# Rotary partners of the first block fetched by transfers between partitions, and the probabilities of a unit turned after the next unit's scores

## The reference, cut to what matters

```
u = rms_norm(h, attn_norm[l])
dq, dk, dv, rq, rk, rv, rg, gq, gk, gv, gate_logits = split(u @ w_in[l])
dq = partial_rope(rms_norm(dq, diff_q_norm[l]))     # 4 heads, two maps of 64
dk = partial_rope(rms_norm(dk, diff_k_norm[l]))
rq, rk = apply_rope(rq), apply_rope(rk)             # 4 heads of 128, no norm
gq = axial_rope(rms_norm(gq, gqa_q_norm[l]))        # 8 query heads of 64
gk = axial_rope(rms_norm(gk, gqa_k_norm[l]))        # 2 key heads of 64
# apply_rope(x): [x1*c - x2*s, x2*c + x1*s], x1 and x2 the halves of x
# partial_rope: only the first 16 of 64 features; axial_rope: 32 by row, 32 by column
```

## Time and profile before

| | us |
|---|---|
| median of three runs | 3668.25 (3666.96 to 3669.92) |
| profiled execution, own time | 3669.73 |
| its span, first to last instruction | 3667.9 |
| mean granted TensorE clock | 0.997 of 2.4 GHz |
| PE busy | 3579.5 (98%) |
| DVE busy | 1718.9 (47%) |
| ACT busy | 1390.4 (38%) |

### The profile page before, as it was taken

The page is one execution under the profiler, slowest core; times in us unless marked ns, Lnnn a source line. Parts: engine busy times, 40 slices in busy tenths (PEclk is TensorE's granted clock), DMA queues, the critical chain, the costliest instruction groups (busy, mean ns, idle before and its releaser), DMA issues.

```text
span 3667.9 us, 47289 instructions
## 1 busy us (share of the span) xinstructions
PE 3579.5 (98%) x18053; PEld 2684.7 (73%) x18053; DVE 1718.9 (47%) x2498; ACT 1390.4 (38%) x2056; POOL 2.4 (0%) x9
## 2 busy tenths in 40 slices
PE   8999999999999999999999899999999999999999
PEld 5565788777775656887777764488888885368998
DVE  5664434434456754344333545543333355644334
ACT  4554323322245543233222334533323334443334
POOL 0000000000000000000000000000000000000000
PEclk9999999999999999999999999999999999999999
DMA  3111233555531112334565320012222222013332
GB/s 113 46 46 41 71 96 92 155 149 143 156 91 46 47 41 69 92 111 135 161 174 149 91 66 3 2 51 64 63 63 63 63 78 72 3 46 97 93 92 86
DMA packets 571967, 304.71 MB, mean 83 GB/s; under 512 B 26592, under 2 KB 565552, under 8 KB 571824
## 3 DMA queue, kind: packets, MB, share of 16 engines
q1 hardware_dynamic: 571168, 302.41, 29.0%
q10 hardware_dynamic: 656, 0.33, 0.0%
HBM read 299.55 MB, written 2.10 MB: 82 GB/s over the span
## 4 chain that ended last, share of the span: by engine, by line
PE 94%; ACT 2%; DVE 2%; issue 1%; DMA 0%; SPq 0%; DVEq 0%; ACTq 0%
PE ps L1085 14%; PE ps L1087 14%; PE ps L1086 14%; PE ps L1404 10%; PE ps L1406 10%; PE ps L1408 10%; PE ps L1597 2%; PE ps L1579 2%; PE ps L1254 2%; PE ps L1285 2%; PE ps L1169 1%; PE ps L1266 1%; PE ps L1238 1%; PE ps L1538 1%; PE ps L1282 1%
## 5 line engine op out<-in xcount | busy, mean ns | idle before, releaser
L1761 ACT ACTIVATE whi<-wraw 128x1024 fp32r<-128x1024 f32 x448 | 470.7, 1051 | 545.9 <-DMA wraw<-in_w_mlp 247.1
L1085 PE MATMUL ps<-uhi,whi 128*128 128x512 f32 (+1 forms) x1456 | 626.2, 430 | 12.1 <-DVE ulo L2413 5.0
L2396 DVE TENSOR_TENSOR wlo<-wraw,whi 128x1024 fp32r<-128x1024 f32 x448 | 546.0, 1219 | 117.4 <-ACT whi L1761 112.7
L1086 PE MATMUL ps<-ulo,whi 128*128 128x512 f32 (+1 forms) x1456 | 572.8, 393 | 0.0
L1087 PE MATMUL ps<-uhi,wlo 128*128 128x512 f32 (+1 forms) x1456 | 572.7, 393 | 0.0
L1085 PEld LDWEIGHTS ps<-uhi,whi 128*128 128x128 f32 x1456 | 274.4, 188 | 136.0 <-issue 71.3
L1086 PEld LDWEIGHTS ps<-ulo,whi 128*128 128x128 f32 x1456 | 274.8, 189 | 77.3 <-issue 22.8
L1087 PEld LDWEIGHTS ps<-uhi,wlo 128*128 128x128 f32 x1456 | 274.0, 188 | 65.4
L1404 PE MATMUL ps<-u2hi,whi 128*128 128x512 f32 (+1 forms) x1216 | 295.5, 320 | 3.6 <-DVE wlo L2396 2.4
L1404 PE MATMUL ps<-yhi,whi 128*128 128x512 f32 (+1 forms) x976 | 295.7, 353 | 0.0
L1408 PE MATMUL ps<-yhi,wlo 128*128 128x512 f32 (+1 forms) x976 | 295.0, 353 | 0.0
(11 more groups left out here) (323 smaller groups left out, 4629.0 us busy)
## 6 DMA issues: line engine op xcount, KB each, us to landing
wraw<-in_w_in SPq DMA_DIRECT2D x128, 512.0 KB, 3.8
wraw<-in_w_mlp SPq DMA_DIRECT2D x128, 512.0 KB, 4.0
mod_raw<-in_w_mod SPq DMA_DIRECT2D x96, 512.0 KB, 5.3
wraw<-in_w_mlp_in SPq DMA_DIRECT2D x64, 512.0 KB, 4.3
wraw<-in_w_mlp_out SPq DMA_DIRECT2D x64, 512.0 KB, 3.9
wraw<-in_w_branch SPq DMA_DIRECT2D x16, 512.0 KB, 3.4
wraw<-in_w_out SPq DMA_DIRECT2D x16, 512.0 KB, 3.8
wraw<-in_w_o SPq DMA_DIRECT2D x16, 512.0 KB, 3.8
```

Of the source, the lines that this page charges most:

```text
L1085: pe.matmul(bank, whs[:, i], x_hi[:, k], start=(i == 0), stop=False)
L1086: pe.matmul(bank, whs[:, i], x_lo[:, k], start=False, stop=False)
L1761: act.activation(whi[:, r], wraw[:, r], ACT.Copy).then_inc(w_hi, 1)
L2396: dve.tensor_tensor(wlo[:, r], wraw[:, r], whi[:, r].bitcast(F32), ALU.subtract).then_inc(w_split, 1)
```

## The change

For each rope, PE's "rotate" step and its permutation matrices are gone. When ACT has copied a projection to `rawb`, SP sends the partner features to a new tile `rotated` by transfers between partitions: 4 transfers of 8 partitions for a diff rope, 4 of 32 for a gqa rope (whose features are now ordered so that row and column parts lie together), 2 of 64 for a ret rope. They stand in SP's program behind the load of the weight chunk four places on. SP first waits for the copy and, because there is one tile `rotated`, for the rope before to be finished.

Normed ropes are reordered on DVE: gain and cosine on `rawb`, swapped gain and signed sine on `rotated` ("head_scale", now at end + 3.1, two instructions), then their sum, then the multiplication by the root ("roped", now at end + 3.7). Plain ropes keep three DVE instructions at end + 2.4 instead of end + 0.9, and read the partners from `rotated` instead of from a bank. One small transfer (`gain_swapped`) comes first among the parameters, and POOL clears `rotated` once per layer.

The other part of the change moves "turn" from place + 2.6 (+ 3.3 for the second) to + 2.9 (+ 3.6), which is behind the score step of the next unit (at + 2.85); "turned" and "attend" move along.

```
+SWAPS = [[(at + n * (1 - half), at + n * half, n) for at in starts for half in range(2)]
+         for starts, n in (((0, 64), 8), ((0,), 64), ((0, 64), 32))]
...
     def turn_about(end, r):
...
-            put(at + 0.9, "head_scale", rope=r)
-            at += 2
-        put(at, "rotate", rope=r)
-        put(at + 0.4, "roped", rope=r)
+            at += 2.3 if end == ends[0] + 1 else 0
+            put(at + 1.6, "head_scale", rope=r)
+            at += 2.2
+        else:
+            at += 1.9
+        put(at, "roped", rope=r)
...
             for m in range(2 if kind == "gqa" else 1):
-                s = put(at + 2.6 + 0.7 * m, "turn", score=unit, index=m)
-                put(at + 2.9 + 0.7 * m, "turned", head=s, score=unit, index=m)
-        at += 4.2
+                s = put(at + UNIT_SPACE + 0.05 + 0.7 * m, "turn", score=unit, index=m)
+                put(at + UNIT_SPACE + 0.35 + 0.7 * m, "turned", head=s, score=unit, index=m)
+        at += UNIT_SPACE + 1.45
...
+                def rotations(chunk):
+                    if chunk not in ropes_of:
+                        return
+                    r = ropes_of[chunk]
+                    bank_done(sp, bank_evac, r.tile)
+                    sp.wait_ge(rope_done, r.rot)
+                    sp.wait_ge(rotated_clear, l + 1)
+                    for to, start, n in SWAPS[r.table]:
+                        sp.dma_start(rotated[to:to + n, :], rawb[start:start + n, r.n % 2, :]).then_inc(rot_in, 16)
...
                             column_chunk(whole.chunk, a["w_in"][l], whole.columns)
+                        rotations(whole.chunk - RAW)
...
-                    elif step.name == "rotate":
-                        r = step.rope
-                        if r.normed:
-                            pe.wait_ge(qn_ready, r.norm + 1)
-                        else:
-                            bank_done(pe, bank_evac, r.tile)
-                        bank_wait(pe, aux_free, r.rot_aux)
-                        src = rawb[:, r.n % 2]
-                        pe.matmul(ps[:, AUX + r.rot_aux % 2], mats[:, r.table, :], src, start=True, stop=True)\
-                            .then_inc(rot_done, 1)
...
                     elif step.name == "head_scale":
                         r = step.rope
-                        inverse_root(r.root)
                         bank_done(dve, bank_evac, r.tile)
-                        dve.scalar_tensor_tensor(rawb[:, r.n % 2], rawb[:, r.n % 2], par[:, r.gain:r.gain + 1],
-                                                 root[:, r.root % 2], ALU.mult, ALU.mult).then_inc(qn_ready, 1)
+                        dve.wait_ge(rot_in, 16 * r.rot_in)
+                        src, swapped = rawb[:, r.n % 2], r.gain - ROW["diff_q_norm"]
+                        dve.scalar_tensor_tensor(src, src, par[:, r.gain:r.gain + 1], ropes[:, 2 * r.table], ALU.mult,
+                                                 ALU.mult)
+                        link(dve.scalar_tensor_tensor(rotated[:, :], rotated[:, :], gain_swapped[:, swapped:swapped + 1],
+                                                      ropes[:, 2 * r.table + 1], ALU.mult, ALU.mult))
                     elif step.name == "roped":
                         r = step.rope
+                        src = rawb[:, r.n % 2]
                         if r.normed:
-                            dve.wait_ge(qn_ready, r.norm + 1)
+                            link(dve.tensor_tensor(t1, src, rotated[:, :], ALU.add))
+                            inverse_root(r.root)
                         else:
                             bank_done(dve, bank_evac, r.tile)
-                        src = rawb[:, r.n % 2]
-                        link(dve.tensor_tensor(t1, src, ropes[:, 2 * r.table], ALU.mult))
-                        dve.wait_ge(rot_done, r.rot + 1)
-                        dve.tensor_tensor(t2, ps[:, AUX + r.rot_aux % 2], ropes[:, 2 * r.table + 1], ALU.mult)\
-                            .then_inc(aux_free[r.rot_aux % 2], 1)
-                        bank_done(dve, aux_free, r.rot_aux)
+                            link(dve.tensor_tensor(t1, src, ropes[:, 2 * r.table], ALU.mult))
+                            dve.wait_ge(rot_in, 16 * r.rot_in)
+                            link(dve.tensor_tensor(t2, rotated[:, :], ropes[:, 2 * r.table + 1], ALU.mult))
...
-                        dve.tensor_tensor(dst, t1, t2, ALU.add).then_inc(rope_done, 1)
+                        if r.normed:
+                            dve.tensor_tensor(dst, t1, root[:, r.root % 2], ALU.mult).then_inc(rope_done, 1)
+                        else:
+                            dve.tensor_tensor(dst, t1, t2, ALU.add).then_inc(rope_done, 1)
```

More of the change, by code:

```diff
@@ L107, in rope @@
     def rope(dst, slot, table, hd=None, gain=None):
-        return Step("rope", dst=dst, slot=slot, table=table, hd=hd, gain=gain)
+        r = Step("rope", dst=dst, slot=slot, table=table, hd=hd, gain=gain)
+        r.normed = gain is not None
+        return r
     def turn_about(end, r):
@@ L222, in number_steps @@
             if s.use in ("normed", "plain"):
-                s.rope.n, s.rope.tile, s.rope.normed = num["rope"](), s.tile, s.use == "normed"
+                s.rope.n, s.rope.tile = num["rope"](), s.tile
             if s.use == "normed":
@@ L234, in number_steps @@
             s.rope.root = num["root"]()
-        elif name == "head_scale":
-            s.rope.norm = num["normed"]()
-        elif name == "rotate":
-            s.rope.rot_aux, s.rope.rot = num["aux"](), num["rot"]()
         elif name == "roped":
             r = s.rope
+            r.rot = num["rot"]()
+            r.rot_in = num["rot_in"](len(SWAPS[r.table])) + len(SWAPS[r.table])
             r.free_after = 0 if r.hd is None else last.get(("scored", r.hd - 2), 0)
@@ L503, in __init__ @@
             "rank_normed "
-            "gqa mean split final gate norm norm_tile mlp_tile residual x_turn").split()}
+            "gqa rot_in mean split final gate norm norm_tile mlp_tile residual x_turn").split()}
         last = {"value_turn": -1, "swish_tile": -1, "final": -1}
@@ L676, in build @@
         decay = sb("decay", [P, TOEPLITZ], scope=head_scope)
+        rotated = sb("rotated", [P, SEQ], scope=head_scope)
         head_scope.close()
@@ L751, in build @@
         shifts = sb("shifts", [P, 2, 2])
+        gain_swapped = sb("gain_swapped", [P, 4 * DEPTH])
         token_root = sb("token_root", [P, 4])
@@ L976, in half_chunk @@
                     sp.dma_start(view[1], second).then_inc(raw_in[r], 16)
+                ropes_of = {step.chunk: step.rope for step in s.heads if step.name == "project" and step.rope}
+                def rotations(chunk):
[7 more added lines that the diff above has]
+                        sp.dma_start(rotated[to:to + n, :], rawb[start:start + n, r.n % 2, :]).then_inc(rot_in, 16)
                 for step in s.heads:
@@ L1001, in _ @@
                                          w.rearrange("(k p) c -> p k c", p=P)).then_inc(raw_in[r], 16)
+                        rotations(step.chunk - RAW)
                     elif step.name == "gate":
                         column_chunk(step.chunk, a["w_in"][l], GATES + D * step.n + P * step.d)
+                        rotations(step.chunk - RAW)
                 for j in range(KT):
@@ L1136, in small_products @@
                 pe.wait_ge(small_sums, 1)
-                pe.matmul(ps[:, SCORE + 1, 0:4], mats[:, 4, :], small[:, 16:20], start=True, stop=True)\
+                pe.matmul(ps[:, SCORE + 1, 0:4], mats[:, 1, :], small[:, 16:20], start=True, stop=True)\
                     .then_inc(par_turned, 1)
@@ L1290, in _ @@
                         bank_wait(pe, aux_free, step.aux)
-                        pe.matmul(ps[:, AUX + step.aux % 2], mats[:, 4, :], fo[:, :], start=True, stop=True)\
+                        pe.matmul(ps[:, AUX + step.aux % 2], mats[:, 1, :], fo[:, :], start=True, stop=True)\
                             .then_inc(mean_done, 1)
@@ L1295, in _ @@
                         bank_wait(pe, aux_free, step.aux)
-                        pe.matmul(ps[:, AUX + step.aux % 2], mats[:, 4, :], fsq[:, :], start=True, stop=True)\
+                        pe.matmul(ps[:, AUX + step.aux % 2], mats[:, 1, :], fsq[:, :], start=True, stop=True)\
                             .then_inc(fsq_used, 1)
@@ L1974, in _ @@
                         act.wait_ge(sq_used, r.sq + 1)
[L1975 removed]
+                        root_of(r.root, r.sum_aux, 64, NORM_EPS, (rope_done, r.rot + 1))
                     elif step.name == "value_turned":
@@ L2376, in small_parameters @@
                     link(dve.tensor_scalar(c, c, factor, None, ALU.mult))
+                for at in (0, 2 * DEPTH):
+                    link(dve.tensor_scalar(gain_swapped[:, at:at + DEPTH], gain_swapped[:, at:at + DEPTH], 64 ** -0.5, None, ALU.mult))
                 dve.wait_ge(small_exp, 2)
@@ L3027, with swapped, axes_apart @@
 SECOND_DMAS = 5
-PARAM_DMAS = 11 + 2 + 1 + 8 + 4 + 4
```

(16 more changed lines are left out.)

35 lines of the change are left out of this document (18 added, 17 removed).

## The result

| | before | after |
|---|---|---|
| median | 3669.09 us (3666.96 to 3670.05, 4 runs) | 3633.63 us (3632.98 to 3636.19, 4 runs) |
| profiled span | 3667.9 us | 3632.3 us |
| mean granted clock | 0.997 | 0.997 |

A forecast was written before the change was run, and what follows sets the result against it. PE, busy 98% of the span, was taken as the bound. Terms -36.1 - 2.8 - 7.7 - 5.1 - 2.0 + 7.8 + 1.6 + 3.8 sum to -40.5 us, so 3668.25 becomes 3628 us, range 3612 to 3651.

The forecast's parts named there:

- The rotates: On PE in the attention stage: 42 rotates at 0.86 us each leave, -36.1 us, with 43.8 as upper bound.
- waits ahead of rotates: PE's waits for DVE ahead of rotates go together with the rotates, -2.8 us.
- behind copies: PE's turns waiting for the bank behind a copy (3.5 and 1.6 us) no longer wait, -5.1 us.
- Waits for probabilities: PE's turns waiting for weighed probabilities: 3.4 us left in place of 11.1, -7.7 us.
- New neighbours: Steps now touching in one bank on PE: ten pairs of turns +7.8 us, two value turns touching a diff turn +1.6.
- gqa value turn and attend: One value turn and one attend per layer wait for the second "turned" behind ACT's exponentials: +3.8 us, bounds 0 and 8.
- the attend's move: One attend per layer on PE depends on the later second "turned" in gqa units: 0.7 us more each, within the +3.8.
- Transfers taken at 0: Partner transfers on SP land before DVE wants them, covered by 2.0 us or at worst 0.4: no cost.
- Rival 3: Partners come late at DVE's wait on `rot_in`, passed on to PE from 0.96 us per rope: 3678 at 1.2; chance 0.05.
- Rival 1: Waits moved, not removed: eight DVE ropes cost PE 1.5 us each, new neighbours wait twice as long; 3649, chance 0.22.
- the turns' move: Turns on PE put behind the next scores: shorter waits against new neighbours and gqa order, -1.6 us net.
- Rival 4: Longest new waits of PE bring the 1.2 GHz clock, adding 4 to 8 us: 3634, inside the forecast's 0.58 chance.

The follow-up runs named there:

- the doubled rotates: Kernel before with each of the 42 rotate products issued twice into the same bank: 3702.81 us, ratio 1.0098 to the kernel before.
- The parted turns: Changed kernel with the attend step back at + 4.2 and the ten touching pairs of turns parted: 3628.01 us, on another chip 3624.21 us.
- ropes alone: Changed kernel with turn, turned and attend steps at their old places, new transfers and rope order kept: 3657.65 us, ratio 0.9970 to the kernel before.
- cut transfers: Changed kernel with every transfer of partners cut into two halves along the tokens: 3653.06 us, ratio 0.9956 to the kernel before.
- turns alone: Kernel before with turn, turned and attend steps moved as in the change, rotates kept: 3661.72 us, ratio 0.9982 to the kernel before.
- the kernel with more products: Changed kernel with turns at their old place and the product summing a normed rope's squares issued twice, 26 more products: 3671.80 us.

## Why the prediction was right, and where its steps were off

The forecast of 3628 (3612 to 3651) against 3633.6 was right in sign and size, and inside its range. The main mechanism, rotates leaving a busy PE, is as forecast; that the total came so near is in part luck. The sum had -4.4 us for all waits together and the rows give +4.8 (39.1 against 34.3), 9.2 us worse. Some 4 us of PE's own time that the sum did not have were gained by the new order. By its own steps:

- **The rotates** (-36.1): right; the doubled rotates give 34.5.
- **The waits ahead of rotates** (-2.8), **behind copies** (-5.1), **of retention scores** (-2.0): gone, gone, and -2.7.
- **Waits for probabilities** (-7.7): mis-sized by 1.8; 5.2 us are left, not 3.4, and over the sign that the prediction named (below 4). For the first unit the working gave 1.2 to 1.3 and the trace shows 1.02, but six more waits of up to 1.0 stood in units to which I gave 0.4 per layer.
- **New neighbours** (+7.8 + 1.6): all there to the number (7.9 and 1.6). The parted turns show the first to be worth 9.6: the price was the wait in the row, not the time from start to start.
- **gqa value turn and attend** (+3.8): +1.8 and +2.7 come to 4.5.
- **The step that was off most: the attend's move**, taken at +0.7 per layer for PE alone. What I left out is ACT's order behind it: moved by 0.1 place, "attended" of the last pair fell behind the copy of a projection whose end was 6 us off. +6.0 in the trace; undone, 6.7 by medians and 4.2 by spans. It is two thirds of the 9.2 us by which the waits were off; another 1.2 us are waits of the last norms for ACT's `fsq` (they are there with ropes alone too), which the sum did not have either.
- **Transfers taken at 0**: right for this kernel (7.7 us of DVE's waits, nothing of it traced on to PE beyond the 5.2), with a cover of about 1 us and not 2.0. Rival 3 put the price of lateness as "passed on to PE, from 0.96 us per rope on"; cut transfers passed on 19.4 / 42 = 0.46 us per rope, mostly at the first unit of each layer and by the clock.
- **Rival 1** (waits moved, 1.5 us for each of eight ropes) is wrong for the changed kernel. Something like it happens with the ropes alone: 27.6 us of waits in 24 places. So the term that the sum had for the turns' move, -1.6 net, hides what it did: with the new ropes on DVE it is worth 3657.65 - 3633.63 = 24.0 us (two chips), without them 6.6. With it the rotates can go without waits opening in their place.
- **Rival 4** (clock): nothing in the changed kernel (10.2 us before, 10.3 after), some 8 us in the ropes alone and 7 in the cut transfers.

The waits and the rotates at 0.82 give -34.4 + 4.8 = -29.6 of the -35.6 between the two spans. The rest lies in PE's work by starts. Take each stretch of PE's other work in the attention stages, from its start to the start of the second projection product behind it, less 0.23 us and without waits. All stretches together fall from 309.9 to 269.5 us, and -40.4 + 4.8 = -35.6. The rotates are 36.1 of the 40.4, at 0.86 each. The other 4.3 (up to 1 of it is the clock) come from the new order: turn, scores and the return to projections take 69.88 - 67.96 - 0.23 = 1.69 us before, while scores, turn and the return take 107.06 - 105.27 - 0.23 = 1.56. Before, 42 turns stood directly ahead of scores, and now none does. With turns alone the same count falls by 5.0 us, which with the waits (31.1 against 34.3) and the clock (7.1 against 10.2) makes up the -11.5 between those spans.

What stays open: no kernel with the ropes split on DVE as before the change, and none with products added where the rotates stood, was run, so the two halves of the waits with ropes alone are counted from the traces and not tested one by one.

## What to carry to other kernels

Price the parts of a change together where one engine's order and another's slack meet: work taken off the bound engine shows its gain only if what it then waits for was given room in the same step. When a step is moved by a tenth of a place in a hand-written order, read on each engine what it falls behind, above all an instruction that waits for something long. And price a wait between two neighbours from start to start of the work around it, not from the wait's row.

## What the runs showed of the hardware

The same stall does not always bring the lower clock. With ropes alone, 2.08 us of idle PE ahead of 68.29 were followed by half the clock (1.98 us for a score step of 1.13); in the kernel with more products, the same place has the same wait of 2.08, the same 2.92 busy of 5.00 us, and a granted clock of 1.00. Over runs this goes with spread: for the ropes alone the fastest run (3653.36 us) has a mean granted clock of 0.997 and the slowest (3663.14) 0.993. The Trainium skill ("TensorE: Matmul & The Clock Gate", section on how oscillation bites) has long idle gaps throttle the engine again; the wait of 4.05 us, with a granted clock of 0.50 behind it, agrees, while the waits of 2.08 us, halving the clock in one kernel and not in another, do not follow from the gap alone.

A wait's row is less than what it costs: 0.78 us in the row, 1.05 from the start of the pair to the start of the next product, since the record of the turn before it reaches 0.25 us past the point where the next product starts if nothing waits (0.66 us long, next product 0.41 later, in the parted pair). The Trainium skill ("Perfetto Trace Analysis", section on the Tensor Engine instruction) says that the profiler estimates a matmul's end; the trace agrees.

The order of short steps on PE has a price of its own, with no wait in it: a turn ahead of scores takes 1.69 us to the return of the projections' pace (67.96 to 69.88 before), behind them 1.56 (105.27 to 107.06 in the parted version), each less 0.23.
